# Attention of a hybrid diffusion layer: four transposes freed from the output copy, the fifth moved behind their copy

## What is computed

```python
def one_block(qblk):                      # 128 queries, 8 heads, two score maps c per head
    s = jnp.einsum('bqhcd,bkhcd->bchqk', qblk, k).astype(jnp.float32) * scale
    p = jax.nn.softmax(s, axis=-1)
    a = p[:, 0] - lam * p[:, 1]
    return jnp.einsum('bhqk,bkhv->bqhv', a.astype(v.dtype), v)
```

## Time and profile before

| what | value |
|---|---|
| median of 3 runs | 1475.68 us (1473.54 to 1480.54) |
| the profiled execution, its own device time | 1474.83 us |
| its span, first to last instruction | 1473.1 us |
| TensorE busy (matmuls) | 1378.2 us, 94% |
| VectorE busy | 389.9 us, 26% |
| ScalarE busy | 228.0 us, 15% |
| the two attention loops | about 192.8 to 271.1 us, and 409.1 to 487.3 us of the span |

### The profile page before, as it was taken

The page is one execution under the profiler, slowest core; times in us unless marked ns, Lnnn a source line. Parts: engine busy times, 40 slices in busy tenths (PEclk is TensorE's granted clock), DMA queues, the critical chain, the costliest instruction groups (busy, mean ns, idle before and its releaser), DMA issues.

```text
span 1473.1 us, 11868 instructions
## 1 busy us (share of the span) xinstructions
PE 1378.2 (94%) x4780; PEld 709.2 (48%) x4781; DVE 389.9 (26%) x783; ACT 228.0 (15%) x449; POOL 143.0 (10%) x149
## 2 busy tenths in 40 slices
PE   5999988899988899999999999999969999999995
PEld 1444345444255455555555555554544444444442
DVE  0321057321067711211000000004661232232232
ACT  3211045211055100000200000002111011011010
POOL 0132000132000000000000000000010222222221
PEclk9999999999999999999999999999979999999998
DMA  9511430011520001303100510053167988988961
GB/s 349 210 58 65 171 122 1 15 57 65 205 88 1 0 1 57 115 0 114 58 1 0 200 57 0 0 190 153 58 230 277 362 325 331 367 328 331 342 244 55
DMA packets 93346, 206.38 MB, mean 140 GB/s; under 512 B 8880, under 2 KB 9200, under 8 KB 93296
## 3 DMA queue, kind: packets, MB, share of 16 engines
q1 hardware_dynamic: 80864, 184.16, 34.1%
q0 software_dynamic: 12000, 20.48, 3.8%
q10 hardware_dynamic: 432, 1.05, 0.2%
HBM read 205.61 MB, written 23.10 MB: 155 GB/s over the span
## 4 chain that ended last, share of the span: by engine, by line
PE 87%; DVE 5%; DMA 3%; ACT 3%; issue 1%; SPq 0%; POOL 0%; POOLq 0%; DVEq 0%; ACTq 0%
PE psum L1283 33%; PE psum L1388 14%; PE psum L1195 14%; PE psum L1406 7%; PE psum L1165 5%; PE psum L1310 4%; PE psum L1267 3%; PE psum L1244 2%; PE psum L1260 2%; DMA arena<-rows_scratch 1%; DMA x<-in_x_prompt 1%; DVE arena L824 1%; PE psum L1379 1%; DVE softmax_stats L850 1%; ACT arena L644 1%
## 5 line engine op out<-in xcount | busy, mean ns | idle before, releaser
L1283 PE MATMUL psum<-arena,weight_ring 128*128 128x128 f32 (+1 forms) x1792 | 487.6, 435 | 1.7 <-ACT arena L678 1.7
L1283 PEld LDWEIGHTS psum<-arena,weight_ring 128*128 128x128 f32 x1792 | 271.4, 192 | 217.8 <-issue 217.8
L1388 PE MATMUL psum<-weight_ring,arena 128*128 128x512 f32 x512 | 224.3, 596 | 0.0
L1195 PE MATMUL psum<-weight_ring,arena 128*128 128x512 f32 x480 | 209.8, 593 | 2.0 <-ACT arena L589 1.5
L1388 PEld LDWEIGHTS psum<-weight_ring,arena 128*128 128x128 f32 x512 | 97.0, 192 | 115.9 <-issue 115.9
L563 ACT ACTIVATE arena<-psum 128x512 f32<-128x512 f32 (+4 forms) x84 | 49.6, 597 | 594.8 <-PE psum L1283 431.3
L1195 PEld LDWEIGHTS psum<-weight_ring,arena 128*128 128x128 f32 x480 | 89.5, 190 | 106.6 <-issue 104.3
L1406 PE MATMUL psum<-arena 128*128 128x512 f32 x256 | 112.6, 593 | 0.7 <-ACT arena L713 0.7
L1165 PE MATMUL psum<-weight_ring,silu_c 128*2 128x512 f32 x192 | 86.2, 604 | 16.2 <-DMA weight_ring<-in_w_ada 16.2
L492 POOL DMA_INDIRECT arena<-h_scratch,slot_tokens x16 | 15.4, 961 | 747.5 <-DVE slot_tokens L1054 742.9
L1310 PE MATMUL psum<-weight_ring,arena 128*128 128x512 f32 x160 | 73.7, 610 | 3.9 <-DVE arena L939 2.1
(11 more groups left out here) (200 smaller groups left out, 800.8 us busy)
## 6 DMA issues: line engine op xcount, KB each, us to landing
weight_ring<-in_w SPq DMA_DIRECT2D x32, 2048.0 KB, 12.7
weight_ring<-in_w_in SPq DMA_DIRECT2D x16, 2048.0 KB, 8.2
arena<-in_w SPq DMA_DIRECT2D x16, 2048.0 KB, 12.1
weight_ring<-in_w_ada SPq DMA_DIRECT2D x12, 2048.0 KB, 8.4
weight_ring<-in_w_conv_out SPq DMA_DIRECT2D x2, 2048.0 KB, 7.7
weight_ring<-in_w_attn_out SPq DMA_DIRECT2D x2, 2048.0 KB, 7.8
arena<-rows_scratch SPq DMA_DIRECT2D x8, 512.0 KB, 7.6
weight_ring<-in_w_o SPq DMA_DIRECT2D x2, 2048.0 KB, 7.7
```

The costliest lines, as they stand in the source:

```text
L1195: last = mm(ps[:, 0:512], hT[:, k, P * i:P * (i + 1)], w[:, k, :], start=(k == 0), stop=(k == KT - 1))
L1283: last = mm(ps[:, lo:hi], w[:, k, P * (n % 4):P * (n % 4 + 1)], src[:, k, lo:hi], start=(k == 0), stop=(k == KT - 1))
L1388: last = mm(psum[:, 1024 + 512 * j:1536 + 512 * j], xgT[:, t, :], w[:, t, :], start=(t == 0), stop=(t == KT - 1))
```

## The change

On TensorE only tiles 0 to 3 are transposed in the first step, into bank 6, and that step no longer waits for o_copy(n-1); `s_aTp` now counts after these. After scores(n+3) and the wait for the copy of those tiles, the fifth tile is transposed into the first 128 columns of bank 6, and signals `s_lastTp`. The wait for o_copy(n-1) now stands before the value product, which has bank 7 alone. Before tile 4 of the value product there is a new wait for `s_lastT`.

On ScalarE, probs_T copies 512 columns rather than 640 for a latent item. A new copy, last_probs_T, of 128 columns stands between the two exponentials of item n+2 (or alone, in the two iterations in which there is no such item). Context items keep their one transpose and one copy. VectorE's program is unchanged.

```diff
@@ ScalarE
                     act.wait_ge(s_aTp, n + 1)
                     if n - 20 * g >= 2:
                         act.wait_ge(s_pv, n - 1)
-                    w = KEYS if i < CTX else N_CTX
+                    w = N_LAT if i < CTX else N_CTX
                     A(aT[n % 2][:, 0:w], psum[:, 3072:3072 + w], ACT.Copy).then_inc(s_aT, 1)
+
+                def last_probs_T(n):
+                    act.wait_ge(s_lastTp, n + 1 - n // NT)
+                    A(aT[n % 2][:, N_LAT:KEYS], psum[:, 3072:3072 + N_CTX], ACT.Copy).then_inc(s_lastT, 1)
...
                         for c in range(2):
+                            if c == 1 and m >= 2 and (n - 2) % NT < CTX:
+                                last_probs_T(n - 2)
                             last = A(prob[n % 2][:, c, 0:w], S[:, KEYS * c:KEYS * c + w], ACT.Exp, bias=st[:, c:c + 1],
                                      accum_out=st[:, 4 + c:5 + c])
                         last.then_inc(s_exp, 1)
+                    elif (n - 2) % NT < CTX:
+                        last_probs_T(n - 2)
@@ TensorE
                     pe.wait_ge(s_mix, n + 1)
-                    if m >= 1:
-                        pe.wait_ge(s_o, n)
-                    for j in tiles:
+                    for j in tiles[0:4]:
                         last = tr(psum[:, 3072 + P * j:3072 + P * (j + 1)], amix[n % 2][:, P * j:P * (j + 1)], ident[:, :])
                     last.then_inc(s_aTp, 1)
                     if m + 3 < items:
                         scores(n + 3)
                     pe.wait_ge(s_aT, n + 1)
+                    if i < CTX:
+                        tr(psum[:, 3072:3200], amix[n % 2][:, P * 4:P * 5], ident[:, :]).then_inc(s_lastTp, 1)
+                    if m >= 1:
+                        pe.wait_ge(s_o, n)
                     for j in tiles:
+                        if j == 4:
+                            pe.wait_ge(s_lastT, n + 1 - n // NT)
                         vt = v_sb[:, j if i < CTX else 5, P * h:P * (h + 1)]
                         last = mm(psum[:, 3840:3968], aT[n % 2][:, P * j:P * (j + 1)], vt, start=(j == 0), stop=(j == len(tiles) - 1))
```

More of the change, by code:

```diff
@@ L293, in build @@
         s_scores, s_max, s_exp, s_mix = sem("scores"), sem("maxes"), sem("exps"), sem("mixed_probs")
+        s_lastTp, s_lastT = sem("last_probs_transposed"), sem("last_probsT_copied")
         s_aTp, s_aT, s_pv, s_o = sem("probs_transposed"), sem("probsT_copied"), sem("pv_done"), sem("o_copied")
```

## The result

The changed kernel is faster: a median of 1457.13 us against 1474.88 us, 17.8 us less; the ratio is given as 0.9873 with a 95% interval of 0.9846 to 0.9901 (that of the two medians is 0.9880). A second comparison of the same two kernels gave 1458.24 us against 1473.34 us, 15.1 us less, a ratio of 0.9896 (0.9878 to 0.9914). The forecast was 1462.9 us with a range of 1459.5 to 1470.0, so the direction was right and the gain too small: 12.8 us were forecast, 15 to 18 us came.

What follows compares the result with a forecast made beforehand. TensorE, busy 94% of the span, was taken as the bound. Three heads at 1.45 us plus a last at 2.03 give 6.4 a loop, 12.8 for two: 1474.83 to 1462.0, forecast 1462.9 us, range 1459.5 to 1470.

Steps and rivals of the forecast that it cites:

- the rest of the kernel as it was: Outside the two attention loops: unchanged, so the first loop's 6.4 us shift should carry to the end.
- the step from rows 4 to 0.59 us: One head's TensorE timeline: with the value product 1.33 us in the stream, the transposes start 0.59 us late.
- a full item (i=2): Third latent item of a head: no wait for the late copy, 3.38 us, a gain of 0.58.
- i=0: First latent item of a head: TensorE's own work decides, 3.38 us for 3.97, a gain of 0.59.
- the new ring: Late copy, last product tile, o_copy, max, exponential: 3.41 us beside TensorE's own 3.38, replacing a ring of 3.97.
- i=1: Second latent item of a head: waits for the late copy until 2.98, about 3.43 us for 3.45, gain 0.02.
- i=3: Fourth latent item of a head: 0.10 charged at tile 4 for the late copy, 3.48 us, gain 0.49.
- the context item: Last item of a head (i=4): VectorE bounds, next transposes need its mix; 3.14 us for 2.91, loss 0.23.
- the 0.17 of cover for the scores behind the exponentials: Second exponential and its sum done by about 3.75, scores(n+4) needing them start at 3.92: cover 0.17, thin.
- The broken stream: Rival: two new TensorE waits each cost a 0.22 us restart per latent item, about 1475 us; no change, chance 0.07.
- The ring at full latencies: Rival: full-length members and 0.15 us hand-overs give 4.33 against 3.97, 8 us slower, 1483; slower, chance 0.04.
- the likeliest case: Whole kernel: a gain of 8 to 15 us, chance 0.73.

Runs made afterwards that it cites:

- the met waits: The changed kernel with a long-met wait for mix added ahead of each tile of every value product: 1457.83 us in the one run.

## Why the prediction was right, and where it failed

**Right: what is removed, and that it carries.** The wait for o_copy was nine tenths of the worth of a head (experiment with the wait put back), and nothing behind the loops took the gain back.

**Two steps failed.** The measured median lies 5.8 us under the forecast. Of these 2.6 us are the size of the pause and of the product in the sum (next paragraph), 0.8 us are that the median of before is 1474.88 and not 1475.68 with one more run, and 2.4 us are left for the rest of the span, which the prediction took as fixed ("the rest of the kernel as it was") and for which its range had no term. With the first step put right the forecast is 1460.3 us, inside the range, and counted from the better median 1459.5, on its edge; what carried the time out of it is the second. Against the 15.1 us of the second comparison nothing is left to explain, so part of the miss is chance.

**Wrong: the size of the pause, the step from rows 4 to 0.59 us.** The prediction took a value product as 1.33 us in the stream, which is its recorded 1.38 less 0.05; other neighbours there overlap by 0.06 and 0.07 (scores and what stands beside them). No row of before shows a product followed at once by something, so this was a guess where a bound was due, and it stood in the sum as if read. Measured: behind a fifth transpose the next transposes start 1.12 after the product does (218.75 to 219.87), 0.16 ahead of its recorded end (220.03). With the same 0.16 the product of before ends 1.22 in the stream, and the pause was 222.64 - 221.94 = **0.70**, not 0.59, as long as the one measured with the wait put back. Together with 0.07 less for a product that starts behind a transpose rather than behind scores (product 1.12 for 1.22, transpose 0.17 for 0.13), a full item (i=2) gained 0.76 where 0.58 was summed, and i=0, whose transposes start behind a pause and take 0.05 longer, 0.72 for 0.59. It was in the rows of before in another view: the ten weight loads of this product are recorded at 1.19 us, and one of them takes 0.19 in the mean, which makes (1.19-0.19)/9 = 0.111 from load to load, 1.11 for the product:

```profile
220.72 1.19 PEld L1267 LDWEIGHTS psum<-arena 128*128 128x128 f32 x10 [0.55 <-ACT arena L644]
```

The Trainium skill, "TensorE: Matmul & The Clock Gate", Single matmul latency, gives a single bf16 matmul at full clock 166 ns beyond the time of its columns; in its breakdown, made for the lower clock, the drain is the largest part. The 0.16 us between a recorded end and the next start is as large here, in float32, but it isn't the same everywhere: 0.16 to 0.17 where both neighbours use 128 rows, 0.06 to 0.07 where one of them is the scores with 64. That it is all drain no run shows. The prediction cited that page for another rule and passed this one by.

**Wrong: the rest taken as fixed.** "A shift of 6.4 us should therefore carry to the end" leaves out that TensorE's clock behind pauses differs from run to run. The rest of the span is 1325.6 to 1331.8 us over the profiles, 1328.9 to 1331.8 over those of the kernel before alone. A range around one kernel's time needed some 3 us for this to either side. The runs show the scatter and its means, the lower clock; what decides it in a given run they don't show.

**The sum, corrected.** A head gained 18.26 - 16.53 = 1.73 for 1.45, six times: 1.7 us more. The last heads gained 15.91 - 13.41 = 2.50 in the first loop for 2.03, and the same in the second, 0.9 more. That makes 12.8 into 15.4, which is what the mean of three profiles each shows (143.1 less 127.7). In the three pairs of profiles another 3.3, 3.3 and 5.9 us lie outside the loops, and were not foreseen at all.

**Right: the new ring** (the chain of waits that runs from one o_copy over max, exponential, late copy and last tile to the next o_copy). It was summed at 3.41 us, and the two items that it bounds, i=1 and i=3, take 3.41 each. The profile after has it link by link, here in i=1 of the first head:

```profile
203.55 0.35 DVE L833 TENSOR_SCALAR arena<-psum,softmax_stats 128x128 f32<-128x128 f32 x1 [1.95 <-PE psum L1280]
203.82 1.48 DVE L859 TENSOR_REDUCE softmax_stats<-psum 128x2 f32<-128x1280 f32 x1
205.33 0.79 ACT L667 ACTIVATE arena<-psum,softmax_stats 128x640 f32<-128x640 f32 x1 [0.75 <-DVE softmax_stats L859]
206.12 0.27 ACT L649 ACTIVATE arena<-psum 128x128 f32<-128x128 f32 x1
206.44 0.49 PE L1280 MATMUL psum<-arena 128*128 128x128 f32 x2 [0.58 <-ACT arena L649]
206.96 0.35 DVE L833 TENSOR_SCALAR arena<-psum,softmax_stats 128x128 f32<-128x128 f32 x1 [0.42 <-PE psum L1280]
```

From start to start that is 0.27 + 1.51 + 0.79 + 0.32 + 0.52 = 3.41, each link within 0.01 of its term. That i=1 would gain nothing (0.02 forecast, 0.04 measured) and show a pause for the late copy came true; the pause is 0.58 for 0.4 to 0.5. Its item was forecast at 3.43 with two errors that cancel: o_copy starts 0.20 after the item's first transpose and not 0.09, and the lone pair costs 0.32 to the next transpose and not 0.44. In i=3 the copy costs 0.21 where 0.10 was charged.

**Right in kind, small in size: the context item.** VectorE bounds it, as forecast. It takes 3.26 us, not 3.14, since o_copy starts 0.20 after the next item's transposes, not 0.09: these start 0.16 ahead of the product's recorded end, o_copy 0.04 behind it. Of the 0.17 of cover for the scores behind the exponentials nothing was left: they wait 0.18 in the context item (at 230.34), where mix bounds anyway and it costs nothing.

**The rivals.** The broken stream is refuted by the met waits and by the products of 1.28 us that run over the new wait unbroken. The ring at full latencies is refuted by 3.41, though with one more exponential in it the kernel does turn slower. The bounds of the likeliest case reached 15 us of gain and no further; a sum whose main term was a guess of 0.05 for an overlap of 0.16 should have carried 0.1 an item, 3 us, on that side.

## What to carry to other kernels

The next matmuls can start ahead of a group's recorded end (0.16 us here), so the pause behind it is longer than the idle time on record; take the price in the stream from a place where the next work follows at once, or from the distance between weight loads. When a wait is taken off the critical engine, write down the ring that closes next and its length: here the sum was right to 0.01 us, and it led to the order on VectorE, which was worth another 15 us. Before a total is read as the gain, ask how much of it lies in stretches that the change doesn't touch: here the kernel with the wait put back looked 5.6 us faster than before by its total, and its heads say 0.17 us each. The order of two operations on a helper engine has no sign of its own: max ahead of o_copy cost 7 us while TensorE waited for o_copy, and brought 15 once it didn't.

## What was not expected of the hardware

- A wait on TensorE that is already met costs nothing to be seen: five more in a product left it at 1.28 us recorded and items i=0 and i=2 at 3.25 and 3.19.
- What directly precedes a product matters: 1.38 us recorded behind scores (64 rows), 1.28 behind a transpose (128 rows), by a value product of the same ten matmuls. The next start stands 0.16 to 0.17 ahead of a recorded end between two 128-row groups, 0.06 to 0.07 beside 64-row scores. The cause of either was not tried.
- After the same pause of 1.9 us TensorE ran at a mean clock of 0.91 or 1.00 over the next 20 us, and in three profiles of the kernel before it was 0.91, 1.00 and 0.91; over all profiles the part of the span outside the loops moved by 6 us.
- Within a loop at clock 1.00, a pause of 1.52 us was followed by a stretch of lower clock three times in one loop (a mean of 0.74 over 6.5 us the first time), and not at all in the other.
